# Memory projections with weights split by ScalarE and VectorE, and two norms summed by token columns

## What is computed

```python
def rmsnorm(x, g, eps=NORM_EPS):
    xf = x.astype(jnp.float32)
    y = xf * lax.rsqrt(jnp.mean(xf * xf, axis=-1, keepdims=True) + eps)
    return (y * g.astype(jnp.float32)).astype(x.dtype)

def memory_attn(h, mem_k, mem_v, w_q, w_out):
    q = (h @ w_q).reshape(B, T, MEM_HEADS, MEM_HEAD_DIM)
    ...
    return o @ w_out

    x = x + jnp.concatenate([o_rw, o_mla], axis=-1) @ lp['w_o']
    x = x + memory_attn(rmsnorm(x, lp['g_mem_q']), mem_k, mem_v, lp['w_mq'], lp['w_mo'])
    f, conv_new = conv_ffn(rmsnorm(x, lp['g_ffn']), conv_prev, lp['w_up'], lp['conv_w'], lp['conv_b'], lp['w_down'])
    x = x + f
    ...
    y_prompt = rmsnorm(xp, g_final)
```

## Time and profile before

| | |
|---|---|
| runs | 2478.71 us median of 3 (2476.91 to 2480.27) |
| profiled execution | 2478.8 us, of which the span of the core 2477.2 us |
| TensorE clock, mean granted | 0.948 of full speed |
| TensorE matmul busy | 2261.3 us, 91% of the span |
| TensorE weight load busy | 2091.0 us, 84% |
| VectorE busy | 1323.6 us, 53% |
| ScalarE busy | 665.1 us, 27% |
| GpSimd busy | 151.9 us, 6% |
| query projection | from about 1302.7 to 1406.0 us |
| output projection | from about 1532.9 to 1641.1 us |
| final stage | from about 2450.3 us to the end |

### The profile page before, as it was taken

One profiled execution on the slowest core, in us unless ns is written; L12 is line 12 of the kernel. 1 busy time (PEld: TensorE's weight loads), 2 busy tenths in 40 slices (PEclk: granted clock), 3 DMA queues, 4 the chain that ended last, 5 costly groups with the idle time before them and its releaser, 6 DMA issues. The chain is left out here.

```text
span 2477.2 us, 51907 instructions
## 1 busy us (share of the span) xinstructions
PE 2261.3 (91%) x21128; PEld 2091.0 (84%) x21128; DVE 1323.6 (53%) x2545; ACT 665.1 (27%) x1362; POOL 151.9 (6%) x166
## 2 busy tenths in 40 slices
PE   7999999988868799987998997989999999999984
PEld 6999677766557699984898987989999999999984
DVE  6457444443344555544672243446666666666657
ACT  5110344433243344431130131122211111221111
POOL 0000000005200100000003101300000000000000
PEclk9999999999977899996999987999999999999997
DMA  4111000016322000013002232111111111111102
GB/s 148 49 46 40 32 12 11 6 30 188 101 96 80 31 4 4 4 23 121 22 18 94 76 136 102 35 49 52 52 44 44 35 44 52 44 52 52 43 24 70
DMA packets 81792, 134.11 MB, mean 54 GB/s; under 512 B 27137, under 2 KB 57730, under 8 KB 81442
## 3 DMA queue, kind: packets, MB, share of 16 engines
q1 hardware_dynamic: 70434, 119.22, 15.0%
q0 software_dynamic: 4224, 8.13, 1.2%
q10 hardware_dynamic: 6912, 3.54, 0.5%
HBM read 121.57 MB, written 9.29 MB: 53 GB/s over the span
## 5 line engine op out<-in xcount | busy, mean ns | idle before, releaser
L317 PE MATMUL psum<-high,ff_up 128*128 128x352 f32 x2112 | 518.3, 326 | 12.2 <-issue 6.2
L317 PEld LDWEIGHTS psum<-high,ff_up 128*128 128x128 f32 x2112 | 371.6, 189 | 14.9 <-issue 6.7
L317 PE MATMUL psum<-low,ff_up 128*128 128x352 f32 x1056 | 341.6, 324 | 0.0
L317 PE MATMUL psum<-hid,ff_down 128*128 128x352 f32 x1584 | 260.1, 326 | 12.1 <-issue 12.1
L317 PEld LDWEIGHTS psum<-hid,ff_down 128*128 128x128 f32 x1584 | 258.5, 190 | 12.4 <-issue 12.4
L519 PE MATMUL psum<-h_high,pj_part 128*128 128x352 f32 x960 | 242.4, 330 | 14.9 <-DVE h_low L626 14.9
L317 PEld LDWEIGHTS psum<-low,ff_up 128*128 128x128 f32 x1056 | 199.8, 189 | 0.0
L2988 DVE TENSOR_TENSOR x<-x,psum 128x352 f32<-128x352 f32 x264 | 137.1, 521 | 115.4 <-PE psum L317 115.4
L519 PEld LDWEIGHTS psum<-h_high,pj_part 128*128 128x128 f32 x960 | 172.1, 191 | 20.5 <-issue 10.5
L519 PE MATMUL psum<-h_low,pj_part 128*128 128x352 f32 x480 | 157.5, 328 | 0.0
L2838 ACT ACTIVATE ff_up<-ff_slot 128x1024 fp32r<-128x1024 f32 x44 | 46.2, 1051 | 391.0 <-PE psum L317 384.7
(11 more groups left out here) (412 smaller groups left out, 4452.8 us busy)
## 6 DMA issues: line engine op xcount, KB each, us to landing
ff_slot<-in_w_up SPq DMA_DIRECT2D x44, 512.0 KB, 3.6
ff_slot<-in_w_down SPq DMA_DIRECT2D x22, 512.0 KB, 3.5
pj_slot<-in_w_in SPq DMA_DIRECT2D x20, 512.0 KB, 3.5
mk_slot<-in_w_mkv SPq DMA_DIRECT2D x16, 512.0 KB, 3.8
mz_k<-in_memk SPq DMA_DIRECT2D x8, 1024.0 KB, 5.5
mz_v<-in_memv SPq DMA_DIRECT2D x8, 1024.0 KB, 7.6
ms_keys<-in_lat SPq DMA_DIRECT2D x56, 128.0 KB, 2.7
ms_keys<-in_lat POOLq DMA_DIRECT2D x48, 128.0 KB, 2.9
```

The lines of the kernel that those rows point to most:

```text
L317: mm = pe.matmul(ps, w(a, kk), rhs(b, kk), start=(kk == 0 and n == 0), stop=(kk == nk - 1 and n == 2))
```

## The change

`linear_stage` splits the weights on ScalarE (rounded copy) and VectorE (rest) in place of GpSimd, and its loops are written out. The class `TokenScale` takes RowScale's place in the query projection and in the final stage (the FFN keeps RowScale): 12 matmuls with 88 tokens of `acc` each as the weights and one column of ones as the moving operand sum the squares into a column of 88 partitions for each group; root and reciprocal work on 88x12; and `widen` lays them out again over all partitions, with four matmuls a third whose weights are one such column, broadcast to 128, and whose moving operand is the 88x88 identity. In the query projection the widening comes behind the first tile's products and ScalarE copies it to `acc`; in the final stage VectorE reads it from PSUM. The final output goes out in six transfers of four tiles in place of three of eight. The class Norm, which nothing used, is taken out.

```diff
+class TokenScale:
+    W = C3 // 4
+    def __init__(self, k, name, ctx):
+        self.k, self.S = k, {x: k.sem(f"{name}_{x}") for x in ("sums", "root", "inv", "wide", "copied")}
+        self.col = k.sb(ctx, f"{name}_col", [P, T // self.W])
+    def pe(self, pe):
+        for j in range(T // self.W):
+            mm = pe.matmul(self.k.bank[7][0:self.W, j:j + 1], self.k.acc[:, j * self.W:(j + 1) * self.W], self.k.mask("ones", 1),
+                           start=True, stop=True)
+        mm.then_inc(self.S["sums"], 1)
+    def widen(self, pe, n, bank):
+        W = self.W
+        if n == 0:
+            pe.wait_ge(self.S["inv"], 1)
+        for t in range(4):
+            mm = pe.matmul(self.k.bank[bank][:, t * W:(t + 1) * W], self.col[0:W, 4 * n + t:4 * n + t + 1].broadcast_to([W, P]),
+                           self.k.mask("ident", W, W), start=True, stop=True)
+        mm.then_inc(self.S["wide"], 1)
+    def act(self, act):
+        act.wait_ge(self.S["sums"], 1)
+        act.activation(self.col[0:self.W, :], self.k.bank[7][0:self.W, 0:T // self.W], ACT.Sqrt,
+                       bias=self.k.mask("eps", 1, self.W), scale=1.0 / D).then_inc(self.S["root"], 1)
+    def copied(self, act, n, bank):
+        act.wait_ge(self.S["wide"], n + 1)
+        act.activation(third(self.k.acc, n), self.k.bank[bank][:, 0:C3], ACT.Copy).then_inc(self.S["copied"], 1)
+    def dve(self, dve):
+        dve.wait_ge(self.S["root"], 1)
+        dve.reciprocal(self.col[0:self.W, :], self.col[0:self.W, :]).then_inc(self.S["inv"], 1)
...
-def linear_stage(k, name, w, n_m, groups, H, L, rows=None, prepare=None, nxt=None, first=(), then=(), after=None,
-                 drain_wait=None):
+def linear_stage(k, name, w, ep, H, L, rows=None, nxt=None, then=()):
...
+                for m in range(2, DK):
                     sp.wait_ge(w_low, m - 1)
+                    sp.dma_start(slot[:, m % 2], w[m]).then_inc(w_in[m % 2], 16)
...
-            @block.gpsimd
-            def _(pool):
-                def divide(i, m, j, free=True):
-                    pool.wait_ge(w_in[j], 16 * (i + 1))
-                    if free:
-                        pool.wait_ge(made, 3 * (m - 1))
-                    pool.tensor_tensor(part[:, j, 0], slot[:, j], k.mask("ones", 1).broadcast_to([P, D]), ALU.mult).then_inc(w_high, 1)
-                    pool.wait_ge(w_high, m + 1)
-                    pool.tensor_tensor(part[:, j, 1], slot[:, j], part[:, j, 0].bitcast(F32), ALU.subtract).then_inc(w_low, 1)
...
             @block.tensor
             def _(pe):
+                if norm:
+                    norm.pe(pe)
+                for m in range(DK):
                     pe.wait_ge(w_low, m + 1)
+                    if m >= 2:
+                        pe.wait_ge(taken, m - 1)
                     for n in range(3):
...
+                    if norm and m == 0:
+                        norm.widen(pe, 0, 6)
+                        norm.widen(pe, 1, 7)
+                        pe.wait_ge(norm.S["copied"], 1)
+                        norm.widen(pe, 2, 6)
...
             @block.scalar
             def _(act):
+                def rounded(m):
+                    act.wait_ge(w_in[m % 2], 16 * (m // 2 + 1))
+                    if m >= 2:
+                        act.wait_ge(made, 3 * (m - 1))
+                    act.activation(part[:, m % 2, 0], slot[:, m % 2], ACT.Copy).then_inc(w_high, 1)
+                rounded(0)
+                if norm:
+                    norm.act(act)
+                rounded(1)
+                if norm:
+                    for n, bank in enumerate((6, 7, 6)):
+                        norm.copied(act, n, bank)
+                for m in range(DK):
+                    if m + 2 < DK:
+                        rounded(m + 2)
+                    if nxt:
+                        act.wait_ge(taken, m + 1)
                         nxt.act(act, m)
             @block.vector
             def _(dve):
+                def rest(m):
+                    dve.wait_ge(w_high, m + 1)
+                    dve.tensor_tensor(part[:, m % 2, 1], slot[:, m % 2], part[:, m % 2, 0].bitcast(F32), ALU.subtract).then_inc(w_low, 1)
+                rest(0)
+                if norm:
+                    norm.dve(dve)
+                rest(1)
                 if nxt:
                     nxt.start(dve)
+                for m in range(DK):
+                    for n in range(3):
+                        dve.wait_ge(made, 3 * m + n + 1)
+                        if norm and m == 0:
+                            dve.wait_ge(norm.S["copied"], n + 1)
+                        last = ep(dve, m, n, k.bank[3 * (m % 2) + n][:, 0:C3])
+                    last.then_inc(taken, 1)
+                    if m + 2 < DK:
+                        rest(m + 2)
+                    if nxt:
+                        nxt.dve(dve, m)
...
 def final_stage(k, y):
...
+                for n in range(3):
+                    for i in range(0, DK, 4):
+                        sp.wait_ge(s_full, DK * n + i + 4)
+                        sp.dma_start(third(k.io["o_y"], n)[i * P:(i + 4) * P].rearrange("(k p) t -> p k t", p=P),
+                                     y[:, i:i + 4, n * C3:(n + 1) * C3]).then_inc(s, 16)
+                sp.wait_ge(s, 96)
...
+                norm.pe(pe)
+                for n in range(3):
+                    norm.widen(pe, n, 4 + n)
...
+                norm.dve(dve)
+                for n in range(3):
+                    dve.wait_ge(norm.S["wide"], n + 1)
+                    for i in range(DK):
+                        dve.scalar_tensor_tensor(third(y[:, i, :], n), third(k.x[:, i, :], n), k.vec("g_final", i),
+                                                 k.bank[4 + n][:, 0:C3], ALU.mult, ALU.mult).then_inc(s_full, 1)
```

More of the change, by code:

```diff
@@ L176, in third @@
     return ap[:, n * C3:(n + 1) * C3]
[L179 to L255, removed]
@@ L330, in linear_stage @@
     w_high, w_low, made, taken = [k.sem(f"{name}_{s}") for s in ("w_high", "w_low", "made", "taken")]
[L332 to L338, removed]
     with ExitStack() as ctx:
@@ L341, in linear_stage @@
         part = k.sb(ctx, f"{name}_part", [P, 2, 2, DK * P], FR)
+        norm = TokenScale(k, rows, ctx) if rows else None
         with nc.Block() as block:
@@ L387, in _ @@
[L387 to L407, removed]
-                    if count > 1:
-                        with eng.Fori(0, count // 2) as i:
-                            for a in range(2):
-                                step(2 * i + a, (m0 + a) % 2)
-                    if count % 2:
-                        step(count - 1, (m0 + count - 1) % 2)
-                    m0 += count
+                        products(pe, k.bank[3 * (m % 2) + n][:, 0:C3], lambda a, kk: part[:, m % 2, a, kk * P:(kk + 1) * P],
+                                 lambda b, kk: third((H, L)[b][:, kk, :], n), DK, made)
@@ L429, in _ @@
             @block.vector
             def _(dve):
-                dve.sem_inc(taken, 2)
-                if prepare:
-                    prepare.dve(dve)
-                if rows:
-                    rows.dve(dve)
+                def rest(m):
[4 more added lines that the diff above has]
+                    norm.dve(dve)
@@ L436, in _ @@
+                rest(1)
                 if nxt:
                     nxt.start(dve)
-                drain(dve)
-                if after:
-                    after(dve, made)
+                for m in range(DK):
[9 more added lines that the diff above has]
+                        nxt.dve(dve, m)
@@ L3034, in final_stage, with _ @@
     s, s_full = k.sem("y_out"), k.sem("y_full")
-    rows = RowScale(k, "nfin")
-    with k.nc.Block() as block:
-        @block.sync
-        def _(sp):
-            for n in range(3):
-                sp.wait_ge(s_full, DK * (n + 1))
-                sp.dma_start(third(k.io["o_y"], n).rearrange("(k p) t -> p k t", p=P), y[:, :, n * C3:(n + 1) * C3]).then_inc(s, 16)
-            sp.wait_ge(s, 48)
-        block.scalar(rows.act)
-        block.tensor(rows.pe)
-        @block.vector
-        def _(dve):
-            rows.dve(dve)
-            for n in range(3):
-                for i in range(DK):
-                    dve.scalar_tensor_tensor(third(y[:, i, :], n), third(k.x[:, i, :], n), k.vec("g_final", i), third(k.acc, n),
-                                             ALU.mult, ALU.mult).then_inc(s_full, 1)
+    with ExitStack() as ctx:
+        norm = TokenScale(k, "nfin", ctx)
+        with k.nc.Block() as block:
+            @block.sync
+            def _(sp):
+                for n in range(3):
[4 more added lines that the diff above has]
+                sp.wait_ge(s, 96)
+            block.scalar(norm.act)
+            @block.tensor
+            def _(pe):
+                norm.pe(pe)
+                for n in range(3):
+                    norm.widen(pe, n, 4 + n)
+            @block.vector
+            def _(dve):
+                norm.dve(dve)
[4 more added lines that the diff above has]
```

(1 more changed line is left out.)

27 lines of the change are left out of this document (2 added, 25 removed).

## The result

The changed kernel takes 2463.25 us, median of 6 runs (2459.49 to 2469.57), against 2478.36 (2475.18 to 2483.47, 6 runs) for the kernel before in the same session: ratio 0.994, 95% interval 0.9921 to 0.9958. That is 15 us less, where 6.9 were predicted, and outside the range. The profiled execution is the longest of the six: 2469.57 us, span 2467.9, against 2478.8 and 2477.2 before.

What follows compares the result with a forecast made beforehand. TensorE was taken as the bound, busy in nearly every slice, so other engines count only where it waits. Terms +0.45 - 2.25 - 3.4 - 1.7 = -6.9 us on 2478.8 gave 2471.9 us, range 2468.5 to 2476.4.

Steps and rivals of the forecast that it cites:

- inside the stages: Both projections after their first tile: later splits stay covered by products and written-out loops cost nothing; taken at 0 us.
- The starts: Query and output projections: first weight issue to first product falls from about 8.08 to 5.83 us, 2.25 us gained each.
- Rival B: Starts of both projections: loads or queue set them, not the division, so both keep 8.08 us; 2476.4 us, chance 0.06.
- The widening in the query projection: Behind the first tile's products, 24 passes are pure addition to TensorE: 2.7 us, between 2.0 and 2.7.
- The clock at the two starts: Query start loses up to 0.9 us, output start gains or loses as much; net nothing, +-0.9 in the range.
- The end of the output projection: The last tile has no subtraction behind it, so the stage ends were taken as before, no gain or loss.
- Rival A: Behind the query projection's widening the clock falls and, with a late rise at the start, the time is 2474.2 us; chance 0.22.
- The final chain: Final stage, first sum to first multiply: sums, root, reciprocal and first widening bring the multiply 3.4 us earlier, bounds 1.7 to 5.6.
- The transfers: Final output: six transfers of 704 KB, the last landing 4.0 us after issue instead of 5.5; 1.7 us saved, bounds 1.5 and 2.0.
- Rival C: Final output: the six transfers don't overlap, so the kernel is slower, 2482.2 us, or 2491 at 5.5 us each; chance 0.05.

Runs made afterwards that it cites:

- a_shift65: The changed kernel with 130 satisfied waits (65 instructions) on TensorE ahead of the output projection's first product; 2480.55 us, one run.
- b_final: The kernel before with only the changed kernel's final stage, six output transfers included; 2474.05 us against 2475.66, ratio 0.9987.
- a_shift50: The changed kernel with 100 satisfied waits (50 instructions) on TensorE ahead of the output projection's first product; 2470.92 us, ratio to the kernel before 0.9983.
- a_shift40: The changed kernel with 80 satisfied waits (40 instructions) on TensorE ahead of the output projection's first product; 2459.43 us, one run.
- b_shift40: The kernel before with 80 satisfied waits (40 instructions) on TensorE ahead of the output projection's first product; 2467.78 us against 2476.85, ratio 0.9963.

## Why the prediction was wrong

The direction was right and came from the terms of the sum, but the size was not: the time lay below the range, and more than half of the gain is an effect that the prediction did not hold. That it fell on the good side is luck; with the loop's head at another place the same edit would have lost by it (a_shift65: FFN 814.1 us).

**The step that failed** is one sentence inside the stages: "The hardware loops are written out: ... so nothing is taken for that." It asked what written-out loops cost where they stand, and nothing there did go wrong. It didn't ask what they move. The FFN's loop lies behind them in TensorE's program, and it came to lie 69 instructions ahead of the end of its piece in place of 19: -9.6 us, more than the whole of the sum. The trace of before showed most of it: 6.2 us of "issue" in four gaps, and behind one of them 3.4 us of low clock, another 1.5 us, in the FFN's stretch, which I had read only at its start. The jumps themselves cost 0.5 less in the profile of the changed kernel; the last 1.4 us of the 9.6 are not accounted for. A rival with a price of -6.2 to -7.7 us would have taken the range below the time measured.

**The sum without it.** On the profiled execution the touched stages gave -6.5 us where -6.9 was forecast. Its terms:

- The starts: 2.0 and 2.1 us against 2.25 each. Right, with the earlier trace rows as their model. Rival B falls.
- The widening in the query projection: 2.81 us, taken 2.7 from the earlier trace rows. Right.
- The clock at the two starts: after the first product it is low for 4.2 us in place of 2.9, and for 3.3 in place of 4.8 (+0.6 and -0.7 by 0.45 us for each), within the +-0.9. The output start's gain holds in all traces: 3.3 to 3.9 us at the low clock in the kernels with the new code whose start is not delayed, 4.8 to 5.1 in the three with the old. That the query start lost by the change isn't shown: the old code has 2.9, 3.0 and 6.2 us there in three traces, the new 4.2 to 5.2.
- The end of the output projection was taken "as before". From its last product to the FFN's first issue it is 5.25 us in place of 5.70, -0.45: the last drain starts 0.04 us behind the product and not 0.15, and ScalarE follows it after 0.04 and not 0.23. With this the query projection came out +1.3 (forecast +0.45) and the output projection -3.2 (-2.25).
- Rival A's mechanism, a fall of the clock behind the widening, didn't occur: granted clock 1.00 from 1332 on.
- The final chain: -2.64 against -3.4. The passes were mis-sized. The sums took 0.152 each where 0.131 was scaled from the earlier trace rows (3.65 against 3.2 us), within the bounds given. First widening to first multiply took 2.04 against 1.7: its eight passes took 0.225 each (1.80 us), above the bound of 0.19. The chain as a whole stayed within its bounds (-1.7 to -5.6). Root, reciprocal and hand-over took 0.62 (0.65).
- The transfers: -1.9 for the multiplies and the last landing together against -1.7; the last piece lands 3.6 us after its issue (4.0). Rival C falls: six pieces issued 1.97 us apart land 3.6 us after their issues, so no fixed cost is paid in series here.

What is left between the -16.1 us of the stages and the 15.1 and 15.8 us of the medians is of the size by which untouched stages differ from one profile to another. Why the clock falls ahead of memory attention in nine traces and not in the other two wasn't tried; b_final, with the kernel before's code there, is among the nine.

## What to carry to other kernels

Before a change that adds or removes instructions on an engine, list that engine's idle time of the kind "issue" in every loop behind it, not only beside the change: it can come or go with the place of a loop's head. Look first whether the gap ends just behind another engine's write, as the one of 12.1 us does. Compare kernels only after that is made equal; satisfied waits in a stretch that waits anyway move a loop's head, here 40 instructions for 9 us of the FFN at no cost. Work that lay hidden under a wait (the old norm in the query projection) isn't to be replaced by cheaper work on the bounding engine: 3.86 us of hidden sums were traded for 2.8 visible ones.

## What the runs showed of the hardware

- After a jump back, TensorE goes on with its next 16 KB piece of program no sooner than 2.7 to 3.3 us after the restart, whatever lies between: thirteen products before the gap at 29 instructions, eight at 19, one at 4, and no gap at 69. The piece's packet starts 0.3 to 1.0 us after the restart.
- The jump itself costs 0.6 to 1.2 us in every kernel, without a trend by the distance (2.7 to 4.1 us for the four).
- A stall can bring the granted clock down for 3.4 to 6.8 us more: behind three of the four of 2.2 to 2.4 us in a_shift65, behind one of the four of 1.2 to 1.8 us in before and one of the four of 1.1 to 1.2 us in b_final, behind none of the four of 1.2 to 1.7 us in a_shift50 nor of those of 0.8 us or less in a_shift40.
- VectorE has gaps of this kind too: in b_shift40 6.2 us in three, in each of which a packet of 8192 bytes on the second instruction queue starts 2.0 to 2.2 us ahead of the gap's end. They cost nothing, since the FFN took 798.9 us with them.
- fp32 passes with 88 weight columns and one moving column cost 0.151 and 0.152 us each in the two stages, at half clock; with 128 weight columns and 88 moving, 0.117 at full clock and 0.226 at half.
- A store of 352 KB lands no sooner than one of 704 KB (3.6 and 3.5 us), one of 1408 KB 1.9 us later.
